# Latent attention of one block: scores with opposite sign, and the scaling of the probabilities on GpSimd instead of VectorE

## The reference, cut to what matters

```python
scale = (QK_NOPE + QK_ROPE) ** -0.5
for i in range(s // Q_BLOCK):
    q0, q1 = i * Q_BLOCK, (i + 1) * Q_BLOCK
    sc = (jnp.einsum('bqhd,bkhd->bhqk', q_nope[:, q0:q1], k_nope[:, :q1])
          + jnp.einsum('bqhr,bkr->bhqk', q_pe[:, q0:q1], k_pe[:, :q1])).astype(f32) * scale
    causal = (q0 + jnp.arange(Q_BLOCK))[:, None] >= jnp.arange(q1)[None, :]
    p = jax.nn.softmax(jnp.where(causal, sc, NEG_INF), axis=-1)
    outs.append(jnp.einsum('bhqk,bkhd->bqhd', p.astype(v.dtype), v[:, :q1]))
```

## Time and profile before

| | |
|---|---|
| median of 3 runs | 2206.76 us (2205.31 to 2207.05) |
| the profiled execution | 2206.56 us, of which its span of instructions 2204.8 us |
| TensorE busy | 2170.6 us, 98% |
| VectorE busy | 1713.3 us, 78% |
| ScalarE busy | 1073.4 us, 49% |
| GpSimd busy | 547.2 us, 25% |
| mean granted TensorE clock | 0.997 |

### The profile page before, as it was taken

How to read it: one execution, slowest core, us unless ns; L and a number is a source line. 1 busy time by engine, 2 the same in 40 slices (tenths; PEclk the granted TensorE clock), 3 DMA queues, 4 the chain that set the end, 5 groups by cost and what they waited for, 6 DMA issues and landing times.

```text
span 2204.8 us, 38356 instructions
## 1 busy us (share of the span) xinstructions
PE 2170.6 (98%) x14358; PEld 1895.4 (86%) x14358; DVE 1713.3 (78%) x2889; ACT 1073.4 (49%) x1435; POOL 547.2 (25%) x225
## 2 busy tenths in 40 slices
PE   7999999999999999999999999999999999999997
PEld 6888888888888888899999787888888888888886
DVE  7799788885999688788879666888888874447887
ACT  5555464444555654556545543444444443333454
POOL 4776731118776620210003302100000000000002
PEclk9999999999999999999999999999999999999999
DMA  7555455555555455554454200555555555555564
GB/s 256 186 178 177 159 177 187 191 188 194 186 177 178 152 191 184 183 202 155 168 177 176 77 22 28 202 191 185 182 186 190 190 190 184 184 187 189 190 212 170
DMA packets 69030, 384.73 MB, mean 174 GB/s; under 512 B 15088, under 2 KB 22768, under 8 KB 23984
## 3 DMA queue, kind: packets, MB, share of 16 engines
q1 hardware_dynamic: 68912, 383.09, 49.5%
HBM read 379.89 MB, written 3.18 MB: 174 GB/s over the span
## 4 chain that ended last, share of the span: by engine, by line
PE 68%; POOL 15%; issue 10%; DVE 4%; DMA 1%; ACT 1%; SPq 0%; POOLq 0%; DVEq 0%; ACTq 0%
PE ps L259 33%; PE ps L260 18%; POOL low L241 14%; PE ps L247 3%; PE ps L248 3%; PE ps L249 3%; PE ps L262 2%; DMA raw<-weights_dram 1%; DVE low L234 1%; PE ps L1863 1%; PE ps L1915 0%; PE ps L1907 0%; PE ps L1715 0%; PE ps L1852 0%; PE ps L298 0%
## 5 line engine op out<-in xcount | busy, mean ns | idle before, releaser
L259 PE MATMUL ps<-opA,whi 128*128 128x512 f32 x2460 | 871.2, 394 | 0.0
L260 PE MATMUL ps<-opA,low 128*128 128x256 f32 x2624 | 706.7, 279 | 0.2 <-DVE opA L985 0.2
L229 ACT ACTIVATE whi<-raw 128x2048 fp32r<-128x2048 f32 x346 | 660.3, 1909 | 81.5 <-DMA raw<-weights_dram 80.3
L234 DVE TENSOR_TENSOR low<-raw,whi 128x2048 fp32r<-128x2048 f32 x252 | 583.2, 2315 | 67.2 <-ACT whi L229 51.4
L259 PEld LDWEIGHTS ps<-opA,whi 128*128 128x128 f32 x2460 | 461.0, 187 | 105.9 <-issue 3.0
L241 POOL TENSOR_TENSOR low<-raw,whi 128x2048 fp32r<-128x2048 f32 x95 | 436.6, 4613 | 405.6 <-ACT whi L229 379.2
L259 PE MATMUL ps<-opB,whi 128*128 128x512 f32 x1380 | 494.1, 398 | 14.1 <-DVE opB L418 11.8
L260 PEld LDWEIGHTS ps<-opA,low 128*128 128x128 f32 x2624 | 492.0, 187 | 14.6 <-DVE opA L985 0.5
L260 PE MATMUL ps<-opB,low 128*128 128x256 f32 x1472 | 397.4, 280 | 0.0
L259 PEld LDWEIGHTS ps<-opB,whi 128*128 128x128 f32 x1380 | 259.7, 188 | 77.6 <-DVE low L412 10.5
L268 ACT ACTIVATE crossed<-ps 128x256 f32<-128x256 f32 x168 | 64.6, 384 | 491.6 <-PE ps L262 491.4
(11 more groups left out here) (393 smaller groups left out, 2612.6 us busy)
## 6 DMA issues: line engine op xcount, KB each, us to landing
raw<-weights_dram SPq DMA_DIRECT2D x350, 1024.0 KB, 4.8
bias_t<-table_dram SPq DMA_DIRECT2D x16, 384.0 KB, 6.0
hT<-xT_dram SPq DMA_DIRECT2D x4, 512.0 KB, 9.0
out_dram<-hT SPq DMA_DIRECT2D x3, 512.0 KB, 2.8
lora_g<-lora_dram SPq DMA_DIRECT2D x1, 1024.0 KB, 4.9
p_in<-pT_dram SPq DMA_DIRECT2D x2, 256.0 KB, 5.1
lora_wa<-lora_dram SPq DMA_DIRECT2D x1, 512.0 KB, 5.9
chunk_mats_dram<-compact SPq DMA_DIRECT2D x4, 128.0 KB, 3.2
```

The lines of the kernel that those rows point to most:

```text
L229: act.activation(whi[:, v % RING, :], raw[:, v % RING, :], ACT.Copy).then_inc(hi_done.sem, 1)
L234: v_.tensor_tensor(wlo(v % RING, 0, width), raw[:, v % RING, 0:width], whi[:, v % RING, 0:width].bitcast(F32), ALU.subtract).then_inc(lo_d ...
L259: pe.matmul(*cross, start=start, stop=False)
L260: mm = pe.matmul(ps[:, b, 0:T], wlo(s, w0, w0 + P), op[:, k, 0:T], start=False, stop=False)
```

## The change

Two things are changed in the attention of the second block. First, VectorE scales the scores by `-scale` and subtracts the mask, so that `smm` holds the scores with opposite sign; the minimum of a row is then the bias of the exponential as it stands, the step that negated it goes away, and ScalarE takes its input with `scale=-1.0`. Second, the two multiplications by the reciprocal are now GpSimd's. VectorE raises a new semaphore `over` after the reciprocal, and GpSimd, which waits for it head by head, raises `normed`.

```diff
@@ phase_mla, gpsimd
                 pool.memset(lower[:, 16:32, :], 0.0).then_inc(mx["cleared"].sem, 1)
+                for h in range(MLA_H):
+                    s = st[:, h % 3, :]
+                    pool.wait_ge(*ml["over"](h + 1))
+                    pool.tensor_scalar(smm[:, h % 2, 0, :], smm[:, h % 2, 0, :], s[:, 10:11], None, ALU.mult)
+                    pool.tensor_scalar(smm[:, h % 2, 1:3, :], smm[:, h % 2, 1:3, :], s[:, 11:12], None, ALU.mult).then_inc(ml["normed"].sem, 1)
@@ phase_mla, scalar
-                    act.activation(smm[:, h % 2, 0, :], smm[:, h % 2, 0, :], ACT.Exp, bias=s[:, 4:5], accum_out=s[:, 8:9])
-                    act.activation(smm[:, h % 2, 1:3, :], smm[:, h % 2, 1:3, :], ACT.Exp, bias=s[:, 5:6], accum_out=s[:, 9:10]).then_inc(ml["exps"].sem, 1)
+                    act.activation(smm[:, h % 2, 0, :], smm[:, h % 2, 0, :], ACT.Exp, scale=-1.0, bias=s[:, 4:5], accum_out=s[:, 8:9])
+                    act.activation(smm[:, h % 2, 1:3, :], smm[:, h % 2, 1:3, :], ACT.Exp, scale=-1.0, bias=s[:, 5:6], accum_out=s[:, 9:10]).then_inc(ml["exps"].sem, 1)
@@ phase_mla, vector
-                    link(v.scalar_tensor_tensor(smm[:, h % 2, :, :], ps[:, 1 + h % 3, 0:3 * P].rearrange("p (x k) -> p x k", x=3), scale,
-                                                causal[:, :, :], ALU.mult, ALU.add))
-                    v.tensor_reduce(s[:, 0:1], smm[:, h % 2, 0, :], axis=AX.X, op=ALU.max)
-                    link(v.tensor_reduce(s[:, 1:2], smm[:, h % 2, 1:3, :].rearrange("p x k -> p (x k)"), axis=AX.X, op=ALU.max))
-                    v.tensor_scalar(s[:, 4:6], s[:, 0:2], -1.0, None, ALU.mult).then_inc(ml["biased"].sem, 1)
+                    link(v.scalar_tensor_tensor(smm[:, h % 2, :, :], ps[:, 1 + h % 3, 0:3 * P].rearrange("p (x k) -> p x k", x=3), -scale,
+                                                causal[:, :, :], ALU.mult, ALU.subtract))
+                    v.tensor_reduce(s[:, 4:5], smm[:, h % 2, 0, :], axis=AX.X, op=ALU.min)
+                    v.tensor_reduce(s[:, 5:6], smm[:, h % 2, 1:3, :].rearrange("p x k -> p (x k)"), axis=AX.X, op=ALU.min).then_inc(ml["biased"].sem, 1)
@@ finished
-                    link(v.reciprocal(s[:, 10:12], s[:, 8:10]))
-                    v.tensor_scalar(smm[:, h % 2, 0, :], smm[:, h % 2, 0, :], s[:, 10:11], None, ALU.mult)
-                    v.tensor_scalar(smm[:, h % 2, 1:3, :], smm[:, h % 2, 1:3, :], s[:, 11:12], None, ALU.mult).then_inc(ml["normed"].sem, 1)
+                    v.reciprocal(s[:, 10:12], s[:, 8:10]).then_inc(ml["over"].sem, 1)
```

More of the change, by code:

```diff
@@ L492, in reuse_front_semaphores @@
             over = iter(fr_sigs.values())
-            for signals, names in ((ml, ("scores", "biased", "exps", "normed", "probsT", "probsT_read", "outT", "stored")),
+            for signals, names in ((ml, ("scores", "biased", "exps", "over", "normed", "probsT", "probsT_read", "outT", "stored")),
                                    (wi, ("tok", "tok_read", "sc", "masked", "G", "G_read", "aq", "aq_read", "ry", "ry_read", "mn", "mn_read", "ends", "held")),
```

## The result

| | before | changed |
|---|---|---|
| median of 7 runs each | 2207.26 us (2205.31 to 2208.38) | 2213.13 us (2212.24 to 2214.45) |
| the profiled execution, its span | 2206.56, 2204.8 us | 2213.13, 2211.3 us |
| clearing of `lower` to the next stage's first transposes | 26.36 us | 31.44 us |

The changed kernel is slower: ratio 1.0028, 95% interval 1.0019 to 1.0037, which is 5.9 us, 4.2 to 8.2. Forecast were 2208.3 us, 2204.9 to 2213, and "slower by over 0.2%" had 0.25.

The account below looks back on a forecast made before the run. TensorE was taken to bound the whole kernel, and a VectorE-TensorE ring the attention. 2206.56 + 0.3 (rings) + 1.3 (reload) = 2208.2 us against the profiled execution, stated as 2208.3 us, +0.07%; range 2204.9 to 2213.

Parts of the forecast that it names:

- T: GpSimd's time for a head's two multiplications: 0.73 us, between 0.52 (from clearing) and 0.95 (from products of two tiles).
- That rival: Slower by GpSimd's multiplication in the attention: decides from T = 1.13; at T = 1.5, +7.0 us, 2213.7 us; chance 0.12.
- Its sign of being wrong: What would refute the forecast: a GpSimd TENSOR_SCALAR of 256 columns taking more than 0.62 us, or less than 0.31.
- The ring: Attention's per-head loop, VectorE and TensorE waiting in turn: changes by T - 0.69 us, seven times, +0.3 us.
- negation: VectorE's step between second maximum and reciprocal; dropping it was to save 0.20 us per head.
- handoff: From reciprocal's start to the first multiplication's, now on GpSimd: 0.25 us against 0.19, 0.06 us more per head.
- hiccup: L1806 in the ring took 621 ns once instead of 169; may go or move, +-0.45 us.
- TensorE's own work: TensorE's work per attention head, about 2.53 us, below which no gain could go on (-0.24 a head).
- The end of the stage: Behind head 6 TensorE is the bound; later head 7 covered by 0.87 us, `ends` hidden by 1 us.
- half clock: TensorE's stretch at 1.2 GHz after a standstill: may come once more or go, +-1.6 us, in range only.
- The reload: Row ISA on GpSimd ahead of its first multiplication: fetch lands after 4.4 us, cover 3.2, so 1.3 us late, once.
- The rule that was weighed: Skill's rule on GpSimd elementwise speed: at twice VectorE's time T = 1.10, rings +2.9 us; at line rate -1.0 us.

Follow-up runs that it names:

- probe: Kernel before plus sixteen extra GpSimd instructions behind its clearing; run once, no median given; TENSOR_SCALAR with a column took 0.61 and 0.93 us.
- sign_alone: Kernel before with only the opposite sign and minimum, multiplications left on VectorE; median -2.68 us against before, ratio 0.9978 to 0.9996.
- three_vector: Kernel before with the sign change, multiplications on VectorE, and a third `smm` buffer; median -3.84 us against before, ratio 0.9976 to 0.9994.
- split_blocks: Changed kernel, but VectorE multiplies 256 columns while GpSimd multiplies 128 by TENSOR_TENSOR, second block transposed first; median -2.51 us against before, ratio 0.9983 to 1.0001.
- first_over: Changed kernel with VectorE's reciprocal issued ahead of the next head's mask; median +0.02 us against before, ratio 0.9989 to 1.0007.

## Why the prediction was wrong

**The step that failed** is the one that gave T: "The new instruction reads one tile, halfway between none and two, and I take the middle, T = 0.73." It measured 1.51 us, above even the upper bound of 0.95. The bounds went by how many tiles an instruction reads, and in the probe the copy and TENSOR_SCALAR both read one and write one, at 0.8 and 2.5 ns a column. What GpSimd does in between decides, not what it reads. Of a rival the text itself says what this error costs: "at T = 1.5 it is 7 x 0.81 + 1.3 = +7.0". That rival had 0.12. Its sign of being wrong, over 0.62 us for 256 columns, came with 0.92.

**The ring was right.** T - 0.69 us a head gives +0.82 at T = 1.51, and the masks are 3.58 apart, 2.77 + 0.82 = 3.59. Its parts measured: negation -0.20 (sign_alone), handoff 0.25 us from the reciprocal's start to GpSimd's, GpSimd to TensorE 0.05. Seven heads are +5.7 us. Measured up to the transposes of head 6 are 27.98 us from the clearing, against 22.77 before, +5.21. The difference is, but for 0.1 us, the hiccup of L1806, 0.45 us, which fell away.

**TensorE's own work** was read wrong as well, without effect on the sum: it was put at 2.53 us a head, below which no gain could go, and three_vector shows 2.31.

**The reload** was costed at 1.3 us and is nothing, below 0.1. With the measured T and the assumed reload the sum is 2206.56 + 5.7 + 1.3 = 2213.6; without the reload it is 2212.3. The two errors go opposite ways, and that of T is by far the larger: +5.4 us against -1.3. The first multiplication starts 4.91 us behind the start of the clearing, where 4.96 was forecast for a reload that costs nothing.

**The hiccup** had "nothing there to explain it". It had: I had looked at VectorE and TensorE, and not at GpSimd. In the kernel before, VectorE's and GpSimd's own timelines at 1244 are these:

```profile
1243.94 0.62 DVE L1806 TENSOR_SCALAR st<-st 128x2 f32<-128x2 f32 x1
```

```profile
1243.92 0.62 POOL L1889 TENSOR_TENSOR chunk_ends<-uS,pc 128x256 f32<-128x256 f32 x1
```

Both take 0.62 us at the same time. In sign_alone, which has no L1806, it is the next TENSOR_SCALAR of VectorE at that place that takes 0.60 us instead of 0.29. The probe shows that it is no chance meeting: with GpSimd's instructions added and VectorE's code as before, L1821 (the negation) takes 0.24, 0.33 and 0.41 us instead of 0.17 in the first three heads.

**The end of the stage** went as told: `ends` is ready at 1256.81 and wanted at 1257.68, hidden. TensorE's half clock came at the same place, and the end from the transposes of head 6 on is 0.13 us shorter, so it was no part of the loss. It was costed at 1.6 us; against sign_alone it measured 1.39.

**The rule that was weighed**, about twice VectorE's time for two-input operations, gave 2209.5 us without the reload and would have been the better guide, if still 3.6 us short; T was 2.7 times VectorE's 0.55. As a product of two tiles it is 0.97, 1.8 times, but VectorE's 0.55 is for another instruction. Like against like, the split of a weight unit, a TENSOR_TENSOR of 128x2048, takes 4.61 us on GpSimd (L241) and 2.32 on VectorE (L234) in the kernel before, and there the rule agrees. The Trainium skill's other half of it (GPSIMD Engine Reference, section Engine selection) is that one-input operations run at about line rate: the copy, 0.77 ns a column, can be read so, and TENSOR_SCALAR, also with one tile of input and at 2.5, cannot.

**What is left open.** The stage accounts for 5.07 of the 5.87 us between medians; the rest is within the spread of the runs. In the profiled executions the stage begins 0.97 us later in the changed kernel, but that is decided in the first 22 us, as the next section shows. Why TENSOR_SCALAR is slow on GpSimd was not looked into. Nor is it known what decides whether TensorE falls to half clock at the end of the stage, and whether it does so in every execution of a kernel.

## What to carry to other kernels

Before work moves to an engine that has never run that instruction, the instruction has to be measured there; what an engine takes for clearing, a copy or a product of two tiles does not bound it, and one probe in a hole of the kernel gives the number. In a ring of engines an instruction costs its duration only if it stands in series: moved to a free engine, it hides when what releases it is issued ahead of the work that it is to run beside. Here the same slow multiplication cost 0.8 us a head behind the mask and next to nothing per head beside it. Hidden is not yet a gain: the new order lost at the first and the last head what it won between them, and the kernel with the shortest stage kept the multiplications on VectorE. Of a change in two halves, each half is worth a run alone: the half that helped was hidden by the other one.

## What the runs showed of the hardware

**VectorE's TENSOR_SCALAR is held up by GpSimd, other VectorE instructions here are not.** Beside a running GpSimd instruction it took 0.59 for 0.35 us (split_blocks), 0.62 for 0.17 (before), 0.60 for 0.29 (sign_alone) and 0.54 for 0.29 (probe); GpSimd's own stayed at 0.40 and 0.62 in the first three. Masks, reductions and the copies from PSUM kept their 0.56, 0.41 and 0.41 us beside GpSimd in first_over, at 1240.35 to 1241.88. The Trainium skill, SBUF — State Buffer, section Who interferes with whom, says that VectorE and GpSimd share one pair of ports as an exclusive lock, that `tensor_scalar` is among the instructions which may take it, that a reduction never does on this chip, and that whichever engine issues first gets it and the other waits. That such an instruction is held up and a reduction is not agrees. So does one place in probe: VectorE's L1828 starts at 1233.97 and keeps its 0.34 us, and GpSimd's product of 128 columns, which starts at 1234.05, takes 0.58 us, where the one ahead of it took 0.45. In split_blocks VectorE started 0.04 us ahead of GpSimd and was still the one to wait, which these starts do not explain.

**A stretch at half clock at the start of the program comes in some of the profiled executions and not in others,** independent of what is studied. These are the same 3.6 us in the kernel before and in the changed one (busy us of each engine, granted clock, DMA share, GB/s):

```profile
18.00:21.60 3.60, 3.60 (x21) 2.94 (x20) 3.50 (x6) 3.55 (x3) 0.00 (x0) 1.00 0.94 313
```

```profile
18.00:21.60 3.60, 3.60 (x14) 3.10 (x13) 3.47 (x6) 3.59 (x3) 0.00 (x0) 0.53 0.85 300
```

TensorE goes through 21 products in the one and 14 in the other, and is 1.25 us behind at 50 us. Of the fourteen kernels with a profile, probe among them, eight have this stretch, in places where no instruction differs, so a difference of 1 us between two spans says nothing yet.

**The level that TensorE is granted at the end of this stage is worth 1.4 us,** a fourth of the loss that was measured here: 3.59 us at 1.2 GHz against 2.20 at 2.4 GHz for the same products. Seven of the kernels in the table fell there and six did not. The kernel before and probe have the same code for TensorE and the same 1.55 us of standstill at that place; the one fell (granted clock 0.52 from 1248.0 to 1251.4) and the other did not (1.00 from 1248.4 to 1250.6). So 1.4 us of difference in a stage can come with no difference in what TensorE is given to do, and a comparison has to look at the clock first.
